# Moving the rounded activations of a one-core Trainium2 kernel by 32 bytes in SBUF

## The reference

```python
# first block
h = rmsnorm(x, norm_mix_g); proj = h @ w_in                    # 1024 x 5632
y_a = gated linear recurrence of proj, in chunks of 64         # 8 heads
y_b = cb * causal_depthwise_conv(cc * ch, conv_w)
x = x + (g_a * (y_a @ w_branch_hg) + g_b * (y_b @ w_branch_conv)) @ w_out
h = rmsnorm(x, norm_ffn_g)                                     # expert layer
idx, gate = top 16 of 128 x 128 product keys, 8 heads          # from h @ w_query
x = x + sum over chosen experts of gate * gelu(h . u[idx]) * v[idx]
x = rmsnorm(x, norm_final_g)
# second block, two layers
for layer in (0, 1):
    x = x + 0.5 * swiglu(rmsnorm(x), ffn1)                     # 1024 -> 2816 -> 1024
    x = x + mixer(rmsnorm(x))       # layer 0: stick-breaking attention and pools; 1: block attention
    x = x + 0.5 * swiglu(rmsnorm(x), ffn2)
return rmsnorm(x, norm_final)
```

## Time and profile before

| | us |
|---|---|
| three runs | 2041.24, 2041.58, 2041.86 |
| median | 2041.58 |
| span of the profiled execution | 2039.6 |
| PE busy in it | 2005.6 (98%) |
| DVE busy | 1508.3 (74%) |
| ACT busy | 1123.1 (55%) |

### The profile page before, as it was taken

How to read it: one execution, slowest core, us unless ns; L and a number is a source line. 1 busy time by engine, 2 the same in 40 slices (tenths; PEclk the granted TensorE clock), 3 DMA queues, 4 the chain that set the end, 5 groups by cost and what they waited for, 6 DMA issues and landing times.

```text
span 2039.6 us, 37233 instructions
## 1 busy us (share of the span) xinstructions
PE 2005.6 (98%) x13232; PEld 1822.9 (89%) x13232; DVE 1508.3 (74%) x2564; ACT 1123.1 (55%) x1835; POOL 59.9 (3%) x40
## 2 busy tenths in 40 slices
PE   7999999999999999999999999999999999999998
PEld 6999999988888888888888999999999999999998
DVE  5868898877777777777777667776667667957666
ACT  5445537965555555555555555755555555655554
POOL 0000430000000000000000000000000000000000
PEclk9999999999999999999999999999999999999999
DMA  6445543055565666655665555455555555445553
GB/s 214 135 135 190 205 142 104 24 174 187 189 192 192 187 189 192 191 189 187 206 231 173 187 186 174 135 169 188 187 186 178 185 185 186 156 143 177 185 188 111
DMA packets 101466, 353.73 MB, mean 173 GB/s; under 512 B 11392, under 2 KB 16640, under 8 KB 101120
## 3 DMA queue, kind: packets, MB, share of 16 engines
q1 hardware_dynamic: 100944, 350.13, 52.5%
q10 hardware_dynamic: 432, 2.36, 0.3%
HBM read 348.77 MB, written 3.67 MB: 173 GB/s over the span
## 4 chain that ended last, share of the span: by engine, by line
PE 90%; DVE 7%; ACT 2%; issue 1%; DMA 0%; SPq 0%; DVEq 0%; ACTq 0%
PE front L2030 38%; PE acc L2030 35%; PE tile L2030 16%; DVE w_lo L1219 2%; ACT w_hi L715 1%; DVE rstd L1241 1%; ACT h_parts L741 0%; DMA raw<-stream 0%; PE front L2587 0%; DVE cand L1688 0%; DVE h_parts L1248 0%; DVE sq L1230 0%; DVE conv L1573 0%; DVE rest L1657 0%; DVE top_i L1653 0%
## 5 line engine op out<-in xcount | busy, mean ns | idle before, releaser
L1219 DVE TENSOR_TENSOR w_lo<-raw,w_hi 128x1024 fp32r<-128x1024 f32 x612 | 747.0, 1223 | 85.4 <-ACT w_hi L715 84.9
L715 ACT CAST w_hi<-raw 128x1024 fp32r<-128x1024 f32 x628 | 654.3, 1044 | 137.6 <-PE tile L2030 60.8
L2030 PE MATMUL front<-h_parts,w_hi 128*128 128x512 f32 (+1 forms) x2432 | 586.4, 377 | 4.2 <-ACT h_parts L741 2.5
L2030 PEld LDWEIGHTS front<-h_parts,w_hi 128*128 128x128 f32 x2432 | 436.5, 189 | 80.2 <-issue 2.4
L2030 PE MATMUL front<-h_parts,w_lo 128*128 128x256 f32 x2272 | 337.2, 282 | 0.0
L2030 PEld LDWEIGHTS front<-h_parts,w_lo 128*128 128x128 f32 x2272 | 318.8, 190 | 20.6
L2030 PE MATMUL tile<-h_parts,w_hi 128*128 128x256 f32 x1344 | 247.8, 286 | 5.1 <-DVE w_lo L1219 2.6
L2030 PEld LDWEIGHTS tile<-h_parts,w_hi 128*128 128x128 f32 x1344 | 209.5, 192 | 8.2 <-issue 4.9
L1304 DVE TENSOR_TENSOR scaled<-front,scaled 128x512 f32<-128x512 f32 x76 | 52.6, 692 | 215.1 <-ACT scaled L779 215.1
L2030 PE MATMUL acc<-w_hi,mid_hi 128*128 128x512 f32 x512 | 200.9, 392 | 2.1 <-DVE mid_lo L1793 1.7
L783 ACT ACTIVATE scaled<-scaled 128x256 f32<-128x256 f32 x188 | 78.6, 418 | 223.4 <-DVE scaled L1307 116.6
(11 more groups left out here) (324 smaller groups left out, 2519.5 us busy)
## 6 DMA issues: line engine op xcount, KB each, us to landing
raw<-stream SPq DMA_DIRECT2D x632, 512.0 KB, 3.7
early_u<-stream SPq DMA_DIRECT2D x20, 512.0 KB, 3.6
early_activations<-early_out SPq DMA_DIRECT2D x20, 128.0 KB, 3.5
scaled<-early_activations SPq DMA_DIRECT2D x10, 128.0 KB, 4.0
x<-x_t SPq DMA_DIRECT2D x2, 512.0 KB, 5.3
keysT<-keys_t ACTq DMA_DIRECT2D x1, 1024.0 KB, 6.3
attc<-attention_constants ACTq DMA_DIRECT2D x1, 1024.0 KB, 7.1
out_t<-h SPq DMA_DIRECT2D x4, 256.0 KB, 2.4
```

The source lines that it names most:

```text
L715: nc.scalar.copy(w_hi[:, s, :], raw[:, s, :]).then_inc(hi_ready, 1)
L1219: nc.vector.tensor_tensor(w_lo[:, s, :], raw[:, s, :], w_hi[:, s, :].bitcast(F32), ALU.subtract).then_inc(lo_ready, 1)
L2030: return nc.tensor.matmul(out, lhsT, rhs, start=start, stop=stop, **kw)
```

## The change

`OFF` is 8 floats, 32 bytes. `H_HI` and with it `H_LO` go 32 bytes further on; MID goes 64 bytes further on, `mid_hi` and `mid_lo` 96, and everything from COLS on 128. `raw`, `w_hi` and `w_lo` stay. No instruction is added, removed or put elsewhere in any engine's stream; only addresses differ.

```diff
--- before.py
+++ after.py
@@ -132,10 +132,11 @@
 
 BASE = 16512
 RAW, W_HI, W_LO = 0, RING * D, 2 * RING * D
-H_HI = 3 * RING * D
+OFF = 8
+H_HI = 3 * RING * D + OFF
 H_LO = H_HI + KT * T
-MID = H_LO + KT * T
-COLS = MID + 5 * 2 * T
+MID = H_LO + KT * T + OFF
+COLS = MID + 5 * 2 * T + 2 * OFF
 ONES = COLS + P
 RSTD = ONES + 2 * P
 R_COL = RSTD + T
@@ -263,8 +264,8 @@
         h_hi, h_lo = h_parts[:, 0, :, :], h_parts[:, 1, :, :]
         scaled = sb("scaled", MID, [2, 2 * T])
         hid = sb("hid", MID + 4 * T, [2, T])
-        mid_hi = sb("mid_hi", MID + 6 * T, [2, T], F32R)
-        mid_lo = sb("mid_lo", MID + 8 * T, [2, T], F32R)
+        mid_hi = sb("mid_hi", MID + 6 * T + OFF, [2, T], F32R)
+        mid_lo = sb("mid_lo", MID + 8 * T + OFF, [2, T], F32R)
         cols = sb("cols", COLS, [N_COLS])
         lane = sb("lane", ONES, [2, P])
         ones, iota = lane[:, 0, :], lane[:, 1, :]
```

## The result

The changed kernel takes 2050.99 us (median of four runs, 2049.80 to 2051.84) against 2041.64 us of the kernel before on the same chip: a ratio of 1.0046, 95% interval 1.0032 to 1.0059. The forecast was 2015.2 us and the range 2006 to 2042, so the time lies outside the range and on the other side. It lies on the rival called "Slower", 2050.8 us.

What follows compares the result with a forecast made beforehand. TensorE was taken to bound the kernel. 10848 matmuls x 2.65 ns gave 28.7 us, of which 0.92, 26.4 us, counted, so the median would go from 2041.58 to 2015.2 us; range 2006 to 2042.

Steps and rivals of the forecast that it cites:

- Slower: Rival: the 3648 wide matmuls stay in a burst start's slow rhythm, 8 ns more each; 2050.8 us, chance 0.08.
- What bounds the kernel: TensorE, busy 98% of the span and 90% of the chain; nothing else has to become faster first.
- The factor 0.92: Share of saved TensorE time counted as kernel time, 90/98; 26.4 of 28.7 us.
- The place that already had the layout: `y_hi`, `y_lo` in branch, even_out and w_o, 32 bytes off the grid: 116.7 to 117.8 ns against 120.0 in w_out.
- Nothing changes: Rival: distance from `w_hi`, not the 32-byte offset, spares `y_hi` part of the surcharge; 2041.6 us, chance 0.16.
- First step: `h_parts` goes 32 bytes off the grid; its 5088 matmuls of 256 columns gain 2.65 ns each.
- Second step: `mid_hi`, `mid_lo` go off the grid; 2112 narrow feed-forward matmuls gain 2.65 ns each; 1536 expert ones are wide.
- the `y` price: Gain per 256-column matmul read from the `y` rows against w_out: 2.65 ns in the mean, between 2.2 and 3.3.
- Third step: The 3648 wide matmuls of 512 columns: 2.65 ns gain each taken, with ends from 8 ns more to a gain.
- Fourth step: Everything from `cols` on moves by 128 bytes and keeps its place on the grid: nothing.
- Fifth step: ScalarE and VectorE write `h_parts` and `mid` off the grid: nothing, as earlier writes took alike on and off.
- The loads as a sign: Weight loads beside `h_parts` at 188 ns instead of 192 would show the forecast right.

Runs made afterwards that it cites:

- e11: Against the kernel before, all tiles behind the weights moved by 32 bytes, so `h_parts` and `mid` both lie at 32: 2044.3 us, ratio 1.0015.
- e3: The kernel before with every SBUF tile, weights too, moved 32 bytes further on, all distances kept: 2041.15 us, ratio 1.0001.
- e6: Against the kernel before, all tiles behind the weights moved by 128 bytes: 2047.8 us, ratio 1.0030.
- e8: Against the kernel before, `w_lo` moved by 64 bytes and everything behind it by 512, so only `w_lo` stands apart: 2036.59 us, ratio 0.9979.
- e5: Against the kernel before, all tiles behind the weights moved by 64 bytes: 2029.7 us, ratio 0.9941.
- e10: Against the kernel before, all tiles behind the weights moved by 192 bytes: 2020.0 us, ratio 0.9899.
- e12: `h_parts` and `mid` at distance 0 from the weights in scores' rows, choice and expert loop, at 192 bytes elsewhere: 2019.14 us, ratio 0.9891 to the kernel before.
- e1: Against the changed kernel, `mid` put back on the 64-byte grid, only `h_parts` 32 bytes off it: 2043.24 us, ratio 1.0009.
- e4: Against the changed kernel, offset of 16 bytes instead of 32 (`h_parts` at 16, `mid` at 80 from the weights): 2040.43 us, ratio 0.9998.
- e2: Against the changed kernel, `h_parts` put back on the 64-byte grid, only `mid` 32 bytes off it: 2051.24 us, ratio 1.0050.

## Why the prediction was wrong, step by step

**What bounds the kernel: right.** TensorE's starts are the kernel's time. The factor 0.92 was too simple: the loss of the wide matmuls shows in full, while of the narrow ones' gain of 12.3 us some 2.4 came back as longer breaks, so that a share of 0.80 was left. That the breaks grew because TensorE came early to work that others had still to finish is argued, not shown. Nothing turned on it.

**The place that already had the layout: right as far as it went.** The `y` rows did show 117.5 for 120 because of where `y` lay, and for w_out the same came true. Of the kernel after, one tile in w_out, the row that answers to the first of the earlier trace rows:

```profile
L2031 PE MATMUL tile<-h_parts,w_lo x63: 277/280/284, 194.5 to 216.2; 128*128 128x256 f32 x63
```

21.7 us / (62 x 3) = 116.7 ns. What I read out of it, though, was "32 bytes off the 64-byte grid", and the runs show "32 bytes modulo 256 away from the weights". The prediction had computed the distance, and named it in the rival "Nothing changes" as an alternative cause; it is the cause, but modulo 256, so that an offset of 32 bytes changes it.

**First step, `h_parts` narrow: right.** Steady pairs went from 120 to 117, and the sum is 11.9 us where 13.5 were counted (5088 x 2.65 ns). The difference lies in `front`, whose bursts began at 114 ns even before, so that their mean was 119.2 and not 120, and fell by 2.0.

**Second step, `mid` narrow: failed.** It was to gain 2.65 ns on 2112 matmuls, 5.1 us of the forecast (2112 x 2.65 x 0.92); it gained 0.4 us in all, 0.2 ns each. The step carried the `y` price to `mid` because both were "off the grid". They are at 32 and at 96 modulo 256. With `mid` at 32 the price was right (116.7, e11).

**Third step, the wide matmuls: failed, and this decided the sign.** Between the ends that the rows gave, +8 ns (the start of a burst) and a gain, I took -2.65 ns "because the surcharge is nearly the same for both widths". Measured: 227 to 234 ns in the expert loop, 230 to 233 in the feed-forward layers, +17.4 us over 3648, +4.8 ns each in the mean. A term of 8.9 us of gain (3648 x 2.65 x 0.92) was a loss of 17.4. The 227 ns, too, had been read in the expert loop alone. An equal surcharge at one distance says nothing of how two shapes answer to another distance; no row showed a wide pair there, while the earlier trace rows did show a wide pair in another rhythm, at 235 ns. The trace's own second value was nearer than the analogy. Under "Slower" I had written that the rhythm falls back by itself; at distance 0 it does, at 32 and 96 it does not. From 500 to 1000 us the first five drains of a step take 232 ns in the mean in the kernel before and the last seven 227; in the kernel after all twelve places stand at 231 to 236.

**The rival that came true.** That wide pairs stay in the slow rhythm, the side and the size (2050.8 against 2050.99) were what happened. The reasons that it gave were not shown: in e3 every operand is loaded from off the grid, and in the kernel before each wide `front` matmul changes from `h_hi` to `h_lo` in its stream, and both kernels have those matmuls at 227 ns. The size is partly luck: it has 26.8 us of loss less 17.6 of gain, and measured are 17.4 and 12.3, with 2.4 us of breaks and the clock's 1.5 on top. It had 8 chances in 100, since its only argument against, the fast expert burst, was taken from the very distance that the change leaves.

**Fourth step, the rest keeps its place: nearly right.** `y` stayed on the same place of the 64-byte grid, but went from 32 to 160 modulo 256. Branch, even_out and w_o of the kernel after, in this order:

```profile
L2031 PE MATMUL tile<-y_lo,w_hi x64: 277/280/282, 171.5 to 193.6; 128*128 128x256 f32 x64
```

```profile
L2031 PE MATMUL tile<-y_lo,w_hi x64: 277/280/283, 1336.9 to 1359.7; 128*128 128x256 f32 x64
```

```profile
L2031 PE MATMUL tile<-y_lo,w_hi x64: 277/281/283, 1825.7 to 1848.1; 128*128 128x256 f32 x64
```

22.1, 22.8 and 22.4 us over 63 triples. The second holds a wait for VectorE, 0.65 us from start to start where the kernel before had 0.13. From start to start without breaks the three take 117.3, 117.4 and 118.7 ns, where it was 117.8, 117.8 and 116.7. That costs less than 1 us in all; I had counted nothing.

**Fifth step, writes off the grid: right.** Two rows of the kernel after that answer to the earlier trace rows:

```profile
L742 ACT ACTIVATE h_parts<-x,cols 128x256 fp32r<-128x256 f32 x56 | 24.7, 503 | 32.1 <-DVE x L1409 29.4 <-PE tile L2031 1.7 <-DVE x L1851 1.0
```

```profile
L1331 DVE TENSOR_TENSOR mid_lo<-hid,mid_hi 128x256 fp32r<-128x256 f32 x188 | 78.8, 419 | 0.5 <-ACT mid_hi L790 0.5
```

503 and 419 ns, against 501 and 419. No new wait came up, either: the wide `front` matmuls wait 2.0 us in all for VectorE and others, against 1.6.

**The loads as a sign: misleading.** Loads beside `h_parts` did fall to 189 ns, which I had named as a sign of the gain:

```profile
L2031 PEld LDWEIGHTS tile<-h_parts,w_lo 128*128 128x128 f32 x672 | 127.1, 189 | 0.0
```

They fell to 188 to 190 ns in every kernel that moved `h_parts`, those that lose too (189 in e6, 2047.8 us). In e8 they stayed at 191, although the triples went from 119.9 to 118.1. So the load's recorded length was no measure of the pair's pace.

**What the page says and what was measured.** The Trainium skill, page "SBUF — State Buffer", section "Who interferes with whom", has TensorE waiting on no one; by it, as the prediction read it, e5 to e8 and e10 would all have 2041.6 us. They have 2020.0 to 2047.8 us with nothing changed but distances, so here the measurement decides for pairs of rounded floats: the distance between tiles cost or spared TensorE up to 1%. Whether a port is the reason no run here shows.

**What stays open.** Why 256 bytes, and why the sign of the distance counts: the traces show the starts, not the memory. That a load meets the stream of the matmul ahead of it is argued from their starts (2 to 4 ns apart) and from e8, and was not shown: in e8 all drains moved, not the third that should. Whether the other engines play a part was not tried by a run of its own; the starts of the feed-forward drains (breaks left out) tell some of it. Those without a DMA packet in flight take what all take: 434 of them 120.0 against 120.0 in the kernel before, 406 of them 119.8 against 119.8 in the kernel after. Those during which VectorE and ScalarE both stood still take 120.0 against 120.0 before and 113.6 against 113.4 in e10, but 117.5 against 119.8 after and 120.6 against 118.7 in e6. So DMA traffic does not set the pace; for those two engines it stays open. That a burst has one of two paces was seen (e5, e10, e12); what chooses between them was not found.

## What to carry to other kernels

A price read in one place is good for another only if what sets it is known; where two explanations fit the row (here the grid of 64 bytes and the distance to the weights), move the thing that tells them apart before carrying the price over. Don't give it to another shape because the old costs were alike. Where TensorE is the bound and each matmul has its own load, the distance of the streamed tile from the weights modulo 256 bytes is a free thing to try, at several values and for narrow and wide matmuls apart: here it was worth from +0.5% to -1.1%. Read such a change by starts, group by group: e1 and e4 had times near no change made of two terms of opposite sign.

## What the runs showed of the chip that I had not expected

- The pace of rounded-float pairs depends on the distance between the activations and the weights modulo 256 bytes: 256 columns take 120.0 ns at 0, 116.7 to 118 at 32, 120 at 96 (e2), about 119 at 128 (e6), and at best 113.5 at 64 (e5) and 113.3 at 192 (e10); 512 columns in the expert loop 227 at 0, 233 to 234 at 32 and 96, 229 to 233 at 192. All at a granted clock of 1.00, where the columns alone are 106.7 and 213.3 ns.
- The absolute place did not count at 32 bytes (e3, 1.0001), and the two shapes want different distances: at 0 the wide ones are fastest (227) and the narrow ones as slow as anywhere (120.0).
- At one distance there can be two steady paces (113.3 and 118 ns at 192 in w_in, with `h_parts` and the weights at the same bytes, e10 and e12). A burst there kept the one that it had, and the next could have the other.
- With one offset for all activations, 192 bytes, the kernel takes 2020.0 us, 1.0% less than before; with a place for each stage 2019.1 us, which is the fastest of all that were run and no different from the other within the intervals.
